# Two hybrid blocks on one core: modulation products kept in one PSUM bank and turned once, attention outputs of the first block in the other

## The chip, the cores and the metric

The kernel runs on one core of one Trainium2 chip. Five engines run side by side and wait for each other through semaphores: TensorE (PE, its weight loads are shown as PEld), VectorE (DVE), ScalarE (ACT), GpSimd (POOL) and SyncE (SP), which here only issues DMAs. Matrix products land in PSUM, which has eight banks of 128 partitions by 512 fp32 values. The metric is the device time in microseconds, the median of the runs shown.

## The reference, cut to what matters

Two model blocks run one after the other on 256 tokens of width 1024. The first has two layers of four mixers (compressed, selected and window attention, stick-breaking, gated linear and forgetting attention), gates, an output product and a squared-ReLU network. The second has two layers whose inputs are scaled and shifted by a modulation vector. That vector depends only on `c`, `c_ctx` and weights, so the kernel computes it during the first block:

```
silu_c  = jax.nn.silu(c)          # one row of 1024
silu_cc = jax.nn.silu(c_ctx)      # one row of 1024
mod_lat = (silu_c @ w_ada[i] + b_ada[i])[:, None, :]    # w_ada[i]: 1024 x 6144
mod_ctx = silu_cc @ w_ada[i] + b_ada[i]
```

For each of the two second-block layers that is a product of two rows with a 1024 x 6144 matrix. It is computed during the first-block layer of the same index, as twelve modulation tiles of 512 columns.

## The kernel before

Each engine's program is written by hand, in the order in which it runs; nothing reorders it. The stages of a first-block layer, by the names of the code:

- **Projections.** Weight tiles of 2 MB come through a ring of slots (`W`). For a product in split precision POOL rounds half a tile (`round_high`, L249), DVE makes its low part (`make_low`, L256), and PE does three matmuls per 128 x 128 piece (L268 to L270).
- **The attention loop.** `for m in range(PAIRS + 1)` has 16 pairs of heads, in turn of the kinds slc, win, fox, sb. Iteration m runs on PE `filler(2m)`, `turned(m-1)` (transposes of probabilities L647, or additions L940 for sb), `scores(m)`, `filler(2m+1)` and `output(m-1)`; after an sb pair the second filler comes ahead of the scores. A filler, called a step below (0 to 31), is 24 matmuls of one piece of the gate product, and behind some of them stands a modulation tile.
- **Branches and output product.** 432 matmuls in a row on PE (`branch_part`, then the `wo` products).
- **The transition to the feed-forward network.** Modulation tiles 10 and 11 (`ada_late`), transposes of the normalised x (`turn_x`), then the first `up` product.
- **Feed-forward network.**

**A modulation tile before.** `ada(n)` is 8 matmuls of a 128 x 32 weight (`silu_c`, whose first two columns hold the two rows, the rest is zero) with 512 moving columns. k mod 4 picks one of four groups of 32 PSUM rows, so that the bank holds four partial sums. ScalarE copies the bank to SBUF (`ada_p`, or `ada_gap` for the two late ones). One step later `turn_ada(n)` multiplies four 128 x 128 pieces of that copy by the first two columns of the constant `sum4`, which adds the four partial sums and turns the result into columns: four matmuls with two moving columns each. ScalarE copies eight columns to `mod` (`take_mod`). fp32 operands of this kind take two passes, so that the trace shows 16 and 8 records for 8 and 4 matmuls.

**PSUM.** The banks are used as four pairs: PROJ, SC (scores), PT (transposes) and OT (outputs). A use takes the next bank of its pair in turn, and its `claim` makes PE wait until the use before the last one, which had the same bank, has been read. The modulation tiles and their turns take their turns in PROJ between the gate fillings; only the late turns take OT. The outputs of the attention alternate between the two banks of OT.

**The ring.** In the loop the gate tiles take slots 0 and 1, the modulation tiles slot 2 alone, so the load of a modulation tile starts when the one before has been used. SP issues in one fixed order (`step_tiles`) and waits in it.

```
ada_steps = [i for i in range(4 * KD - 4) if i % 8 in (1, 4, 6)]     # 1 4 6 9 12 14 17 20 22 25
            if i - 1 in ada_steps:
                turn_ada(ada_steps.index(i - 1), ada_p)
            if i in ada_steps:
                ada(ada_steps.index(i))
```

The prologue loads the fp32 constants in one DMA (L1743); `head_sel` is 1024 of their 2143 columns.

## Time and profile before

| | before |
|---|---|
| median of 3 runs | 2328.16 us |
| lowest, highest | 2326.09, 2331.44 us |
| span of the profiled execution | 2320.9 us |
| PE busy in the span | 2218.5 us (96%) |
| DVE, ACT, POOL busy | 1246.1, 691.2, 480.0 us |
| first-block layers, attention loop | 207 to 397 us, 850 to 1040 us |

The runs' median is 7.3 us above the profiled span; that part lies outside the first and last instruction. A row of the timeline gives start and duration of an instruction, or of a run of like ones, and in brackets how long the engine was idle before it and what ended that. Durations of matmuls overlap with the next one; what a matmul costs PE is the distance from its start to the next start.

### The profile page before, as it was taken

The page shows a single profiled execution, that of the slowest core. Times are in us where ns is not written, and L with a number is a line of the kernel's source. Part 1 is how long each engine was busy: PE and PEld are TensorE (multiplying, and loading weights), DVE is VectorE, ACT ScalarE, POOL GpSimd, SP SyncE. Part 2 cuts the span into 40 slices and gives each one's busy share as a digit, 9 for nine tenths or more (in the row PEclk, how much of TensorE's full clock was granted, in tenths as well). Part 3 has the DMA queues.
Part 4 walks back from the last instruction along what each step waited for, and adds up shares of the span by engine and source line. Part 5 has one row for each costly group of instructions (what it writes and reads, how often), then busy time and mean ns, then how long its engine had stood idle before and what let it go on. Part 6 is the DMA issues. An engine that isn't in the chain of part 4 may idle for free.

```text
span 2320.9 us, 33246 instructions
## 1 busy us (share of the span) xinstructions
PE 2218.5 (96%) x13976; PEld 1801.2 (78%) x13976; DVE 1246.1 (54%) x1690; ACT 691.2 (30%) x1531; POOL 480.0 (21%) x259
## 2 busy tenths in 40 slices
PE   7999999999999999999999998899999999998998
PEld 7998788889888987888898644457888885555887
DVE  5675435855455754348554326664433443466666
ACT  2224444032012244440330357622112013272211
POOL 2222112323312211113233000101111110102332
PEclk9999999999999999999999999999999999999999
DMA  9534665645465346556455303022223232122551
GB/s 269 183 118 153 239 228 164 244 146 219 163 188 186 142 145 236 211 189 240 160 208 218 133 0 115 1 73 91 85 97 108 73 84 72 33 100 99 193 196 58
DMA packets 214281, 340.13 MB, mean 147 GB/s; under 512 B 46540, under 2 KB 82359, under 8 KB 214007
## 3 DMA queue, kind: packets, MB, share of 16 engines
q1 hardware_dynamic: 213040, 334.50, 41.4%
q0 software_dynamic: 944, 3.47, 0.5%
q8 instruction: 112, 1.84, 0.3%
q14 instruction: 35, 0.28, 0.0%
q10 hardware_dynamic: 150, 0.04, 0.0%
HBM read 335.90 MB, written 2.10 MB: 146 GB/s over the span
## 4 chain that ended last, share of the span: by engine, by line
PE 56%; DVE 4%; ACT 4%; issue 1%; POOL 0%; DVEq 0%; ACTq 0%; POOLq 0%
PE bank L2091 14%; PE bank L268 13%; PE bank L270 12%; PE bank L269 12%; PE bank L644 3%; PE bank L2094 2%; DVE ring_low L256 1%; ACT work L1111 1%; ACT work L2458 1%; ACT work L2369 1%; DVE cos L2654 1%; PE bank L647 0%; ACT L1111 0%; DVE work L2667 0%; PE bank L940 0%
## 5 line engine op out<-in xcount | busy, mean ns | idle before, releaser
L269 PE MATMUL bank<-hT_high,ring_low 128*128 128x256 f32 (+1 forms) x2048 | 607.6, 297 | 0.0
L269 PEld LDWEIGHTS bank<-hT_high,ring_low 128*128 128x128 f32 x2048 | 392.2, 192 | 11.7 <-issue 0.7
L249 POOL CAST ring_high<-ring 128x2048 fp32r<-128x2048 f32 (+1 forms) x108 | 204.8, 1897 | 707.1 <-PE bank L270 645.5
L268 PE MATMUL bank<-hT_low,ring_high 128*128 128x256 f32 (+1 forms) x1008 | 294.8, 292 | 9.3 <-DVE ring_low L256 4.6
L256 DVE TENSOR_TENSOR ring_low<-ring,ring_high 128x2048 fp32r<-128x2048 f32 (+1 forms) x108 | 242.3, 2245 | 112.5 <-POOL ring_high L249 112.4
L270 PE MATMUL bank<-hT_high,ring_high 128*128 128x256 f32 (+1 forms) x1008 | 287.2, 285 | 0.0
L249 POOL CAST half_high<-ring 128x2048 fp32r<-128x2048 f32 x64 | 129.3, 2024 | 663.4 <-PE bank L270 464.4
L268 PE MATMUL bank<-ring_low,hidden_high 128*128 128x512 f32 x640 | 254.0, 397 | 0.0
L1111 ACT ACTIVATE work<-bank 128x512 f32<-128x512 f32 (+10 forms) x268 | 121.3, 477 | 367.9 <-PE bank L270 314.9
L268 PEld LDWEIGHTS bank<-hT_low,ring_high 128*128 128x128 f32 (+1 forms) x1008 | 192.1, 191 | 19.9 <-issue 12.5
L256 DVE TENSOR_TENSOR ring_low<-ring,half_high 128x2048 fp32r<-128x2048 f32 x64 | 152.7, 2391 | 99.6 <-POOL half_high L249 99.2
L270 PEld LDWEIGHTS bank<-hT_high,ring_high 128*128 128x128 f32 (+1 forms) x1008 | 191.8, 190 | 0.4
L268 PE MATMUL bank<-hT_low,half_high 128*128 128x256 f32 (+1 forms) x528 | 178.7, 338 | 8.3 <-ACT work L2369 3.5
L270 PE MATMUL bank<-hT_high,half_high 128*128 128x256 f32 (+1 forms) x528 | 176.5, 334 | 0.0
L270 PE MATMUL bank<-half_high,hidden_high 128*128 128x512 f32 x384 | 151.5, 395 | 0.0
L269 PE MATMUL bank<-half_high,hidden_low 128*128 128x512 f32 x384 | 150.7, 392 | 0.0
L2091 PE MATMUL bank<-work,ring 128*128 128x512 f32 (+3 forms) x384 | 139.9, 519 | 4.3 <-DVE work L2550 3.4
L2511 ACT ACTIVATE work<-bank 128x512 f32<-128x512 f32 x48 | 28.7, 598 | 385.5 <-PE bank L270 385.5
L268 PEld LDWEIGHTS bank<-ring_low,hidden_high 128*128 128x128 f32 x640 | 120.2, 188 | 26.8
L2091 PEld LDWEIGHTS bank<-work,ring 128*128 128x128 f32 (+2 forms) x384 | 69.4, 183 | 69.3 <-issue 58.5
L2756 DVE TENSOR_TENSOR hidden_low<-work,hidden_high 128x512 fp32r<-128x512 f32 x48 | 36.2, 755 | 157.5 <-ACT work L2514 157.5
L268 PEld LDWEIGHTS bank<-hT_low,half_high 128*128 128x128 f32 x528 | 100.5, 190 | 20.2 <-ACT work L2369 4.2
(239 smaller groups left out, 4483.3 us busy)
## 6 DMA issues: line engine op xcount, KB each, us to landing
ring<-w_ff SPq DMA_DIRECT2D x32, 2048.0 KB, 8.1
ring<-mlp_w SPq DMA_DIRECT2D x32, 2048.0 KB, 7.9
ring<-w_in SPq DMA_DIRECT2D x30, 2048.0 KB, 7.8
ring<-w_ada SPq DMA_DIRECT2D x20, 2048.0 KB, 7.6
ring<-w_branch SPq DMA_DIRECT2D x24, 512.0 KB, 6.2
ring<-w_in SPq DMA_DIRECT2D x32, 256.0 KB, 4.1
ring<-w_out SPq DMA_DIRECT2D x4, 2048.0 KB, 7.6
work<-w_ada SPq DMA_DIRECT2D x4, 2048.0 KB, 13.9
```

The costliest lines, as they stand in the source:

```text
L249: nc.gpsimd.tensor_copy(self.high(i), self.part(i, False)).then_inc(self.high_made, 1)
L256: nc.vector.tensor_tensor(self.part(i, True), self.part(i, False), self.high(i).bitcast(F32), ALU.subtract)\
L268: nc.tensor.matmul(out, a[0], b[1], start=start, stop=False)
L269: nc.tensor.matmul(out, a[1], b[0], start=False, stop=False)
L270: return nc.tensor.matmul(out, a[0], b[0], start=False, stop=stop)
L644: return nc.tensor.matmul(out, lhsT, rhs, start=start, stop=stop)
L1111: return nc.scalar.activation(out, in_, func, **kw)
L2091: return nc.tensor.matmul(o, lhsT, rhs, start=start, stop=stop)
L2094: return nc.tensor.transpose(o, src, ident)
L2369: return f(o, src, ACT.Copy, **kw)
L2511: f(part, ps[:, :].rearrange("p (a b) -> p a b", a=per), ACT.Relu).then_inc(PROJ.free(name), 1)
L2756: vec.tensor_tensor(hidden_low[:, part, 0:n_tok], hidden[:, part, 0:n_tok], hidden_high[:, part, 0:n_tok].bitcast(F32), ALU.subtract).then ...
```

## The change

The twelve modulation tiles of a layer now add into one kept bank. `silu_c` becomes 54 columns wide, with the two rows at columns 22 and 23 and zeros on both sides. Tile n takes as its weight the 32 columns that begin at 22 - 2n, so that the two rows land in PSUM rows 2n and 2n + 1 of each group of 32, and the other rows of that tile add zeros. The bank is copied once (`ada_sums`) and turned once, with 24 moving columns in place of 2, and four copies of ScalarE spread it over `mod`. The ten in-loop turns, their copies and the ten in-loop copies of tiles are gone.

The kept bank is one of OT, so all attention outputs (`outputs`) take the other one. Banks can be placed by name. The gate fillings have PROJ to themselves. The modulation tiles stand behind steps 3, 6, 8, 11, 14, 16, 19, 22, 24 and 27. The slot of a tile is released by a semaphore of its own (`ada_used`), counted by its last matmul as before. The constant `head_sel` is gone: the four matmuls per fox pair that had it as weight read one column of the identity, repeated with step zero.

```diff
-    ada_steps = [i for i in range(4 * KD - 4) if i % 8 in (1, 4, 6)]
+    ada_steps = [i for i in range(1, 4 * KD - 4) if i % 8 in (0, 3, 6)]
...
-               ["go0", "go1"] + [f"o_{k}{c}" for c in range(HALF_HEADS) for k in ("nsa", "fox", "sb")]
-               + [f"adT{n}" for n in ada_late] + ["rows3"] * (l == DEPTH - 1) + ["down2", "down3"])
+               ["go0", "go1"] + outputs + ["ada", "adT"] + ["rows3"] * (l == DEPTH - 1) + ["down2", "down3"],
+               {"ada": 1, "adT": 0, **{name: 0 for name in outputs}})
...
-                        mm(ps[e][:, at:at + n], head_sel[0:8, 2 * c + e, :], fox_row[0:8, 0:n], False, False)
+                        mm(ps[e][:, at:at + n], ident[0:8, 2 * c + e:2 * c + e + 1].to_broadcast([8, P]), fox_row[0:8, 0:n],
+                           False, False)
...
-            thin(PROJ.claim(pe, f"ada{n}"), silu_c, w, KD).then_inc(PROJ.full, 1)
-
-        def turn_ada(n, src, banks=PROJ):
-            ps = banks.claim(pe, f"adT{n}")
-            PROJ.taken(pe, f"ada{n}")
+            ps = OT.open(pe, "ada") if n == 0 else OT.bank("ada")
+            at = SILU_AT - 2 * n
+            for k in range(KD):
+                rows_of = slice(k % 4 * THIN, k % 4 * THIN + THIN)
+                last = nc.tensor.matmul(ps[rows_of, :], silu_c[:, k, at:at + THIN], w[:, k, :],
+                                        start=n == 0 and k < 4, stop=n == MOD_TILES - 1 and k >= KD - 4,
+                                        skip_group_check=True)
+            if n < MOD_TILES - 1:
+                last.then_inc(ada_used, 1)
+            else:
+                OT.close("ada")
+                last.then_inc(OT.full, 1)
+
+        def turn_ada():
+
+            ps = OT.claim(pe, "adT")
+            OT.taken(pe, "ada")
             for c in range(4):
-                last = mm(ps[:, 2 * c:2 * c + 2], src[:, c * P:(c + 1) * P], K("sum4")[:, 0:2], True, True)
-            last.then_inc(banks.full, 1)
+                last = mm(ps[:, c * THIN:c * THIN + 2 * MOD_TILES], ada_sums[:, c * P:(c + 1) * P],
+                          K("sum4")[:, 0:2 * MOD_TILES], True, True)
+            last.then_inc(OT.full, 1)
...
-            if i - 1 in ada_steps:
-                turn_ada(ada_steps.index(i - 1), ada_p)
...
-        for n in ada_late:
-            take(f"ada{n}", ada_gap[:, n % 2, :])
+        ps = OT.arrived(act, "ada")
+        copy(ada_sums, ps[:, :]).then_inc(OT.free("ada"), 1)
```

What stands on PE in a row, first layer, behind step 2 (the 24 gate matmuls that end it are above the first row). L647 and L658 are transposes, banks 0 and 1 are PROJ, 4 and 5 PT. Before:

```order
L647 MATMUL bank1<-consts,work 128x128 [waits out_free1_12,proj_free1_3]
L647 MATMUL bank1<-consts,work 128x128 x3
L644 MATMUL bank0<-consts,work 128x2 [waits proj_free1_3,proj_free0_2]
L644 MATMUL bank0<-consts,work 128x2 x3
L647 MATMUL bank5<-consts,work 128x128 [waits prob_ready_55,turn_free1_9]
L647 MATMUL bank5<-consts,work 128x128 x2
```

Now:

```order
L658 MATMUL bank0<-consts,work 128x128 [waits out_free1_12,proj_free0_2]
L658 MATMUL bank0<-consts,work 128x128 x3
L658 MATMUL bank5<-consts,work 128x128 [waits prob_ready_56,turn_free1_9]
L658 MATMUL bank5<-consts,work 128x128 x2
L658 MATMUL bank4<-consts,work 128x128 [waits prob_ready_56,turn_free0_8]
```

The turn of tile 0 (128x2) is gone, and the transposes of the gated linear output have bank 0, which step 1 filled, in place of bank 1.

On PE in the second layer, at the transition: the last transposes of x, the turns, the turn of the rows for the norms (128x48) and the first `up` matmul. Banks 6 and 7 are OT. Before:

```order
L647 MATMUL bank1<-consts,work 128x128 [waits proj_free1_3]
L647 MATMUL bank1<-consts,work 128x128 x3
L644 MATMUL bank7<-consts,work 128x2 [waits proj_free0_2,out_free1_12]
L644 MATMUL bank7<-consts,work 128x2 x3
L644 MATMUL bank6<-consts,work 128x2 [waits proj_free1_3,out_free0_11]
L644 MATMUL bank6<-consts,work 128x2 x3
L647 MATMUL bank7<-consts,work 128x48 [waits out_free1_12,rows3_in_119]
L268 MATMUL bank0<-hT_low_79,early_high0_75 128x256 [waits hT_cut_121,proj_free0_2,ff_cut_81]
```

Now:

```order
L658 MATMUL bank1<-consts,work 128x128 [waits proj_free1_3]
L658 MATMUL bank1<-consts,work 128x128 x3
L655 MATMUL bank6<-consts,work 128x24 [waits out_free1_12,out_free0_11]
L655 MATMUL bank6<-consts,work 128x24 x3
L658 MATMUL bank7<-consts,work 128x48 [waits out_free1_12,rows3_in_121]
L282 MATMUL bank0<-hT_low_79,early_high0_75 128x256 [waits hT_cut_123,proj_free0_2,ff_cut_83]
```

Two turns became one, and bank 7, on which the rows' turn waits, was last used by a turn before and is last used by the kept bank now.

## Rows read from the trace of the kernel before

**Rows 1.** Windows: both attention loops. Busy us by engine, clock, DMA share, GB/s.

```profile
207.00:397.00 190.00, 185.93 (x1556) 151.78 (x1554) 83.38 (x182) 95.08 (x256) 31.59 (x17) 1.00 0.63 220
850.00:1040.00 190.00, 185.93 (x1556) 151.83 (x1554) 83.38 (x182) 95.21 (x257) 31.46 (x17) 1.00 0.60 208
```

**Rows 2.** Groups by form, PE, loop of layer 1: count, busy us, mean ns, idle before.

```profile
L644 PE MATMUL bank<-consts,work 128*128 128x2 f32 x80 | 9.6, 242 | 0.1
```

**Rows 3.** Timeline, PE: turns of tiles 1 and 3, and what follows.

```profile
240.88 0.95 PE L644 MATMUL bank<-consts,work 128*128 128x2 f32 x8
241.76 0.44 PE L644 MATMUL bank<-work 128*64 128x256 f32 x2
...
268.81 0.95 PE L644 MATMUL bank<-consts,work 128*128 128x2 f32 x8
269.62 0.85 PE L647 MATMUL bank<-consts,work 128*128 128x128 f32 x6
```

**Rows 4.** Timeline, PE: tile 0 and the start of step 2.

```profile
215.03 1.92 PE L644 MATMUL bank<-ring,silu_c 128*32 128x512 f32 x16 [0.39 <-ACT work L1111]
218.48 0.36 PE L268 MATMUL bank<-hT_low,ring_high 128*128 128x256 f32 x1 [1.52 <-ACT work L1111]
```

**Rows 5.** Timeline, PE: modulation tile 2, sb additions behind step 8, step 9, tile 3.

```profile
245.58 1.92 PE L644 MATMUL bank<-ring,silu_c 128*32 128x512 f32 x16
...
257.25 2.02 PE L940 MATMUL bank<-work,consts 128*128 128x256 f32 x12 [0.26 <-DVE work L1602]
259.03 0.36 PE L268 MATMUL bank<-hT_low,ring_high 128*128 128x256 f32 x1
...
262.03 1.92 PE L644 MATMUL bank<-ring,silu_c 128*32 128x512 f32 x16
```

**Rows 6.** Timeline, DVE: first and last operation between scores(4) and their transposes.

```profile
265.06 0.29 DVE L1607 TENSOR_REDUCE work<-bank 128x1 f32<-128x128 f32 x1 [3.69 <-PE bank L644]
...
268.12 0.35 DVE L1617 TENSOR_SCALAR work<-work 128x256 f32<-128x256 f32 x1
```

**Rows 7.** Issue of one modulation tile in the loop: size, us to landing.

```profile
ring<-w_ada SPq DMA_DIRECT2D x1, 2048.0 KB, 7.6
```

**Rows 8.** Timeline: copy of output o_sb0 on ACT, next claim of an output on PE.

```profile
267.32 0.40 ACT L1111 ACTIVATE work<-bank 128x256 f32<-128x256 f32 x1
...
274.48 1.45 PE L644 MATMUL bank<-work 15*64 15x256 f32 x12
```

**Rows 9.** Groups by form, PEld, loop of layer 1: weights of the fox rows.

```profile
L644 PEld LDWEIGHTS bank<-work,consts 8*128 8x128 f32 x32 | 4.4, 185 | 1.6 <-issue 1.3
```

**Rows 10.** Timeline, transition of the first layer: PE and ACT.

```profile
471.01 0.60 ACT L1111 ACTIVATE work<-bank 128x512 f32<-128x512 f32 x1 [0.42 <-PE bank L644]
...
472.15 1.84 PE L644 MATMUL bank<-consts,work 128*128 128x2 f32 x16
...
475.01 0.36 PE L268 MATMUL bank<-hT_low,early_high 128*128 128x256 f32 x1 [1.02 <-DVE hT_low L1408]
```

**Rows 11.** Timeline, transition of the second layer: PE.

```profile
1114.86 1.84 PE L644 MATMUL bank<-consts,work 128*128 128x2 f32 x16
...
1118.67 0.31 PE L647 MATMUL bank<-consts,work 48*128 48x48 f32 x1 [1.96 <-ACT mod L1111]
1118.91 0.58 PE L268 MATMUL bank<-hT_low,early_high 128*128 128x256 f32 x1
```

**Rows 12.** Windows: behind both transitions. Columns as in rows 1; clock third from last.

```profile
476.00:479.50 3.50, 3.50 (x20) 3.50 (x19) 3.50 (x6) 0.00 (x0) 0.00 (x0) 0.57 0.00 0
...
1118.00:1124.50 6.50, 5.83 (x27) 5.77 (x28) 6.09 (x9) 0.80 (x5) 0.00 (x0) 0.51 0.10 38
```

**Rows 13.** The start: load of the constants, first gemm, DMA rate.

```profile
consts<-f_tables SPq DMA_DIRECT2D x1, 1071.5 KB, 6.2
...
17.81 0.58 PE L268 MATMUL bank<-hT_low,ring_high 128*128 128x256 f32 x1 [3.81 <-DVE ring_low L256]
...
3.00:6.00 3.00, 0.00 (x0) 0.00 (x0) 0.00 (x0) 1.28 (x1) 0.00 (x0) 1.00 1.03 401
```

More of the change, by code:

```diff
@@ L141, with __init__ @@
 class Banks:
-    def __init__(self, pair, uses):
+    def __init__(self, pair, uses, places={}):
         assert len(set(uses)) == len(uses)
@@ L149, in __init__, with open, close @@
         pair.uses += len(uses)
-    def bank(self, name):
-        return self.banks[self.order[name] % self.n]
-    def claim(self, pe, name):
-        i = self.order[name]
-        assert i == self.pair.filled, (name, i, self.pair.filled)
-        self.pair.filled += 1
-        if i >= self.n:
-            pe.wait_ge(self.free_sems[i % self.n], i // self.n)
-        return self.bank(name)
+        self.place, self.earlier = {}, {}
+        for name in uses:
+            self.place[name] = b = places.get(name, pair.turn)
+            pair.turn = (b + 1) % pair.n
+            self.earlier[name] = pair.times[b]
+            pair.times[b] += 1
+    def bank(self, name):
+        return self.banks[self.place[name]]
+    def open(self, pe, name):
+        if self.earlier[name] > 0:
+            pe.wait_ge(self.free_sems[self.place[name]], self.earlier[name])
+        return self.bank(name)
+    def close(self, name):
+        assert self.order[name] == self.pair.filled, (name, self.order[name], self.pair.filled)
+        self.pair.filled += 1
+    def claim(self, pe, name):
+        self.close(name)
+        return self.open(pe, name)
     def arrived(self, eng, name):
@@ L1260, in scalar, with take_mod @@
             f(gl_rstd[:, t], gl_stat[:, t], ACT.Exp, scale=-0.5).then_inc(gl_scale, 1)
-        def take_mod(n, banks=PROJ):
-            ps = banks.arrived(act, f"adT{n}")
-            copy(chip["mod"][:, l * (2 * MODC) + 8 * n:l * (2 * MODC) + 8 * n + 8], ps[:, 0:8]).then_inc(banks.free(f"adT{n}"), 1)
+        def take_mod():
+            ps = OT.arrived(act, "adT")[:, 0:4 * THIN].rearrange("p (c q) -> p c q", c=4)
+            mod = chip["mod"][:, l * (2 * MODC):(l + 1) * (2 * MODC)].rearrange("p (n c s) -> p n c s", n=MOD_TILES, c=4)
+            for c in range(4):
+                last = copy(mod[:, :, c, :], ps[:, c, 0:2 * MOD_TILES].rearrange("p (n s) -> p n s", s=2))
+            last.then_inc(OT.free("adT"), 1)
         def filler(i):
```

41 lines of the change are left out of this document (16 added, 25 removed).

## The prediction

> **What bounds the kernel now.** I read the busy time by stretch first. In the two attention loops, where nearly all of the change lies, PE is busy 185.9 of 190 us in both layers, at the full clock (granted 1.00), while DVE has 83, ACT 95 and POOL 32 us of work [rows 1]. The two loops agree to 0.01 us, so whatever is found in one counts twice. Next I read the waits of PE there: what is left idle is a few single waits of 0.3 to 1.5 us [rows 4, 5]. PE's instruction stream is therefore the path; an instruction that leaves it gives back its whole distance to the next start, unless a load or another engine becomes late. I therefore look for two things: which PE work goes, and which waits have lost so much cover that they appear.
>
> The sum is made against the profiled span of 2320.9 us; what lies around it (7.3 us up to the median) contains none of the changed code, so I subtract the same amount from the median.
>
> **1. Ten turns per layer leave the loop.** Their group has 80 records, ten turns of four matmuls in two passes [rows 2]. Its busy 9.6 us counts the tails that overlap with the next matmul, so I take distances between starts: 240.88 to 241.76 is 0.88 us, 268.81 to 269.62 is 0.81 us [rows 3]. Three of the ten in a layer are of the short kind, seven of the long. That is 3 x 0.81 + 7 x 0.88 = 8.6 us a layer, **17.2 us** for two. None of it was idle time. The ten tiles themselves cost as before: same shapes, same count, about 1.85 us from start to next start when undisturbed (a row's 1.92 less the overlap of its tail [rows 5]).
>
> The trace fixes what a two-column turn costs: 0.88 us for eight passes, 110 ns a pass, although only two columns move [rows 3]. The Trainium skill, page "TensorE: Matmul & The Clock Gate", has two rules that bear on it. Its section "Back-to-back issue gap" puts an isolated matmul of up to 64 columns at about 25 ns, by which the twenty turns would be worth 20 x 8 x 25 ns = 4 us, an estimate. Its section "LDWEIGHTS (loading the stationary operand)" puts a weight load at its columns over 1.2 in ns, 107 ns for 128 columns, which gives 17 us; the row agrees with this one.
>
> **2. The first steps wait less.** Before, tile 0 stands behind step 1 and claims the bank of step 0, then step 2 claims that of step 1, and ACT is late with both: PE idles 0.39 and 1.52 us [rows 4]. Now step 2 meets the first wait (0.39, unchanged), and the transposes of the gated linear output meet the second one a gate step later. A step is 3.0 us (259.03 to 262.03 [rows 5], 0.1 of it the change of tile shape). So they are ready at 215.03 + 2.9 = 217.9, and the bank is free about when step 2 starts before the change, 218.48 [rows 4]: 0.5 us of waiting instead of 1.52. That is 1.0 us a layer, **2.1 us** for two. PE now reaches the transposes of pair 0 some 4 us earlier, where DVE's scaling may not be ready; the bound on the low side is half, 1.0 for both.
>
> **3. Three waits behind sb pairs go.** Behind steps 8, 16 and 24 PE waits 0.26 us for DVE [rows 5]. These steps now carry a modulation tile of 1.85 us, while the turn that went ahead of it was 0.88 us, so the cover grows by about 1.0 us, above 0.26. With the tail of the step that shows in such a wait it is 0.3 us each, six of them: **1.8 us**.
>
> **4. What loses cover.** Three places are narrow, and I cost each at nothing.
> (a) Behind steps 10, 18 and 26 there is neither tile nor turn now. The scores end at 265.07; DVE starts at 265.06 and its last scaling ends at 268.47, 3.4 us later [rows 6]. PE wanted the result at 269.62 and will want it 0.81 us earlier, at 268.81 [rows 3]: 0.34 us of cover is left.
> (b) Tiles stand two steps apart at 6 and 8, 14 and 16, 22 and 24, and slot 2 is loaded only after use. Tile 2 of before stands behind step 6 as tile 1 does now: it starts at 245.58 and ends 1.85 us later, and step 8 ends at 257.25 - 0.26 = 256.99 [rows 5]. That is 9.56 us, and without the 0.88 us of the turn between them 8.7 us. The load takes 7.6 us [rows 7] with nothing ahead of it in SP's order. The gate tile is issued behind it, so its bytes follow in the queue. Margin about 1 us; if it failed it would cost the part over 8.7, six times.
> (c) All outputs use one bank. `output(m)` must wait until ACT has copied the output before it. The copy of o_sb0 ends at 267.7, the next output starts at 274.5 [rows 8], and with a turn of 0.81 us less between them 6.0 us of cover stay. ACT also copies an output before it touches the probabilities that the next one needs, so the new wait can never be the last one.
> The fox rows change their weight from eight real columns of a table to one repeated column. Their loads take 185 ns, no more than others of 128 columns [rows 9]; I cost this at nothing, with a bound of double the load, 64 x 0.185 = 12 us worse.
>
> **5. The transitions.** In the first layer PE is ahead of the others: behind the turns it idles 1.02 us, and the `up` product starts when DVE has the low parts [rows 10]. DVE waits there for ACT, which starts on the halves of hT after its copy of the last tile, 471.01 to 471.5 [rows 10]; that copy stays, at the same time. So one turn less gives nothing: its 0.9 us turn into idling. In the second layer the rows' transpose waits 1.96 us for ACT to free the bank of a turn, which ACT does only after all of hT [rows 11]. The bank is now that of the tiles, freed ahead of hT. The `up` product then starts as in the first layer, 475.01 - 472.15 = 2.86 us after the first turn, at 1117.72 instead of 1118.91 [rows 10, 11]: **1.2 us**.
>
> **6. The clock behind the transitions.** After PE had idled 1.02 us the granted clock fell for 3.0 us (0.57 over the window of 3.5, between 2.4 and 1.2 GHz); after 1.96 us it fell for 5.7 us (0.51 over 6.5) [rows 12]. In the first layer PE will now idle about 2.1 us ahead of `up`, like the second before. I take the second layer's case: 2.7 us more at half speed, **a loss of 1.4 us**; the other end is no loss. The second layer keeps its own. The Trainium skill says on the page "TensorE: Matmul & The Clock Gate", section "What's actually happening", that the throttled state is the default and that activity releases it; the trace agrees with its 0.57 and 0.51 behind idle stretches.
>
> **7. The start.** The constants shrink by 1024 of 2143 columns, 512 KB of 1071.5, and move at 401 GB/s: 1.3 us [rows 13]. ACT's first operation waits for them, and from it the chain of squares, norm, transposes and hT leads to the first gemm at 17.81 [rows 13]; the tiles' bytes behind the constants come earlier too. I take **1.3 us**; the low bound is 0.
>
> Sum: 17.2 + 2.1 + 1.8 + 1.2 - 1.4 + 1.3 = 22.2 us, so 2328.2 - 22.2 = **2306.0 us**, 1.0% faster.
>
> **The rivals.**
> *A. The cover is too thin.* PE gives up its work, but waits appear in its place: (b) by 1 us six times, (a) by 0.5 us six times, no gain at the start (1.3), another dip of the clock of 3 us at half speed (1.5). That takes 6 + 3 + 1.3 + 1.5 = 11.8 us: 2318. For it: all margins are under 1 us. Against it: steps 28 to 31 carry no tile or turn already and add only waits as in [rows 5].
> *B. Slower: one bank for the outputs.* There are 24 outputs of which 22 follow another. If ACT fell behind so that each had to wait for the copy of the one before, with a price of 1.2 us (one or two copies of 0.4 us [rows 8] and one more operation of that length in front of them), the loops would lose 26.4 us: 2332. It decides from 1.0 us per output, where it eats the 22.2. Against it stand 6.0 us of cover in (c) and ACT at half load in [rows 1].
> *C. Nothing comes of it.* The turns would only fill holes that something slower makes, a load or POOL's rounding, and the loop keeps its 190 us: 2328.2 less items 5 and 7, plus item 6, 2327. Against it: PE is idle for only 4 of 190 us, with named waits [rows 1, 4, 5].
> *D. More than forecast.* The clock falls less often (the loss of item 6 stays away and one other dip of 3 us goes, 1.4 + 1.5): 2303.
>
> **How the numbers follow.** Forecast with D: 0.84; A: 0.09; B: 0.03; C: 0.04. The forecast with its bounds (start 0 to 1.3, first steps 1.0 to 2.1, clock -3 to +3, (a) and (b) up to 2 together, and the 2.5 us by which the runs themselves differ) reaches from 2299 to 2312; that alone holds 8 in 10, so the range needs none of the rivals. About 0.2% (4.7 us) is what a measurement of this kernel can tell from no change. Faster by more takes the forecast, A and D: 0.93; within it C: 0.04; slower B: 0.03.
>
> **What would show it.** In the profile of the changed kernel: two-column matmuls gone, and one group of 24 columns with 16 records in all; each loop, from its first step to the 432 matmuls of the branches, shorter by 10.5 us; no wait of L940's successor behind steps 8, 16, 24, but still one before the branches; a wait of about 0.5 us in place of 1.52 at the transposes of the gated linear output; no wait for `mod` ahead of the 48-column transpose; a granted clock near 0.5 for about 6 us behind both transitions; the first gemm at 16.5 us. It would be wrong if modulation tiles wait for DMA, if transposes wait for DVE's L1617 in steps 10, 18, 26, if an output waits for ACT's copy, or if the fox rows' weight loads take more than 185 ns.

## The result, and the profile after

| | before | after |
|---|---|---|
| median, first comparison | 2327.12 us (4 runs) | 2294.45 us (4 runs) |
| lowest, highest | 2322.89, 2331.44 us | 2288.33, 2300.05 us |
| ratio, 95% interval | | 0.9859 (0.9837 to 0.9882) |
| span of the profiled execution | 2320.9 us | 2294.1 us |
| instructions of PE, ACT | 13976, 1531 | 13800, 1493 |

The change saves 32.7 us by the medians of this comparison (25 to 36 us by the interval of a second one below). I had predicted 2306.0 us with a range of 2299 to 2312: faster was right, but the time lies 5 us below the range. Before looking for a cause it helps to know the spread: single executions of before lay anywhere from 2315 to 2335 us, so a trace is one draw. I therefore compare the stages over two traces of before and three of after. A ratio below is always to executions of before taken beside the kernel in question.

| stage, mean of its traces in us | before | after | difference | predicted |
|---|---|---|---|---|
| start to first gemm | 17.8 | 17.5 | -0.3 | -1.3 |
| projections, layer 1 | 190.2 | 190.2 | 0 | 0 |
| loop, layer 1 | 189.5 | 178.8 | -10.7 | -10.55 |
| loop, layer 2 | 189.6 | 178.5 | -11.1 | -10.55 |
| branches and output product, both | 131.6 | 131.3 | -0.3 | 0 |
| last `wo` matmul to first `up`, layer 1 | 12.2 | 12.7 | +0.5 | 0 (+1.4 clock) |
| the same, layer 2 | 12.4 | 11.7 | -0.7 | -1.2 |
| first `up` of layer 1 to loop of layer 2 | 375.6 | 373.8 | -1.8 | 0 |
| first `up` of layer 2 to the end | 1204.1 | 1197.4 | -6.7 | 0 |
| sum of the rows | | | -31.1 | -22.2 |

The +1.4 us of clock is my item 6; it is in the predicted sum and was meant to fall behind the first `up`. The loops came out as forecast. Nearly all of the miss lies in the last two rows, nearly all of whose instructions the change does not touch. That is what the experiments had to explain.

The windows of the two loops after, from the first step to the branches (columns as in rows 1):

```profile
209.28:387.97 178.69, 176.64 (x1473) 142.78 (x1473) 88.74 (x182) 87.29 (x233) 31.18 (x17) 1.00 0.63 221
840.45:1018.92 178.47, 176.46 (x1473) 142.67 (x1472) 88.71 (x182) 87.29 (x233) 31.18 (x17) 1.00 0.66 233
```

PE has lost 9 us of busy time against the windows of [rows 1], and it idles 2 us where it idled 4. The groups by form, PE, first of the whole span and then of the loop of layer 1:

```profile
L655 PE MATMUL bank<-consts,work 128*128 128x24 f32 x16 | 1.9, 259 | 0.0
...
L655 PE MATMUL bank<-work 128*64 128x256 f32 x64 | 10.4, 404 | 0.0
```

```profile
L655 PEld LDWEIGHTS bank<-work,consts 8*128 8x128 f32 x32 | 4.4, 184 | 1.6 <-issue 1.3
```

In place of the 80 two-column records of [rows 2] in each loop there are 16 of 24 columns in the kernel. PE never waits ahead of the outputs (128*64): one bank is enough. The fox rows' weight load takes 184 ns, where [rows 9] has 185.

The timeline of PE at the first steps, at step 8, and at both transitions:

```profile
216.84 0.36 PE L282 MATMUL bank<-hT_low,ring_high 128*128 128x256 f32 x1 [0.38 <-ACT work L1134]
...
220.20 1.31 PE L658 MATMUL bank<-consts,work 128*128 128x128 f32 x10 [0.30 <-ACT work L1134]
...
252.78 1.92 PE L1000 MATMUL bank<-ring,silu_c 128*32 128x512 f32 x16
254.63 2.02 PE L952 MATMUL bank<-work,consts 128*128 128x256 f32 x12
...
453.93 1.92 PE L1000 MATMUL bank<-work,silu_c 128*32 128x512 f32 x16
458.41 1.09 PE L658 MATMUL bank<-consts,work 128*128 128x128 f32 x8 [2.55 <-DVE work L1415]
459.43 3.22 PE L1000 MATMUL bank<-work,silu_c 128*32 128x512 f32 x16
...
466.70 0.52 PE L282 MATMUL bank<-hT_low,early_high 128*128 128x256 f32 x1 [1.88 <-DVE hT_low L1430]
...
1093.58 0.97 PE L655 MATMUL bank<-consts,work 128*128 128x24 f32 x8
1094.48 0.26 PE L658 MATMUL bank<-consts,work 48*128 48x48 f32 x1
1096.52 0.36 PE L282 MATMUL bank<-hT_low,early_high 128*128 128x256 f32 x1 [1.78 <-DVE hT_low L1430]
```

The first waits are 0.38 and 0.30 us where [rows 4] has 0.39 and 1.52. The sb additions behind step 8 start without the 0.26 us of [rows 5]. The 48-column transpose no longer waits 1.96 us for `mod` [rows 11], yet the wait ahead of `up` is now 1.78 us.

### The profile page after: what moved, and what is told of

It is laid out like the page before. It is cut to its first block, busy times and chain, and to the rows that moved or that the text cites. A ratio compares the mean times of both kernels' runs of the same rounds, so it can differ in the third digit from the quotient of the medians.

```text
span 2294.1 us, 32812 instructions
## 1 busy us (share of the span) xinstructions
PE 2195.1 (96%) x13800; PEld 1780.6 (78%) x13800; DVE 1259.4 (55%) x1690; ACT 676.0 (29%) x1493; POOL 482.8 (21%) x259
## 4 chain that ended last, share of the span: by engine, by line
PE 56%; DVE 4%; ACT 3%; issue 1%; POOL 0%; DVEq 0%; ACTq 0%; POOLq 0%
PE bank L2113 14%; PE bank L282 13%; PE bank L284 13%; PE bank L283 12%; PE bank L655 2%; PE bank L2116 2%; DVE ring_low L270 1%; PE bank L1000 1%; ACT work L2480 1%; ACT work L2391 1%; DVE cos L2676 1%; ACT work L1134 1%; PE bank L658 0%; DVE work L2689 0%; PE bank L952 0%
## 5 line engine op out<-in xcount | busy, mean ns | idle before, releaser
L1134 ACT ACTIVATE work<-bank 128x384 f32<-128x384 f32 (+11 forms) x246 | 109.4, 466 | 360.8 <-PE bank L284 311.7
## 6 DMA issues: line engine op xcount, KB each, us to landing
work<-w_ada SPq DMA_DIRECT2D x4, 2048.0 KB, 13.2
```

The costliest lines, as they stand in the source:

```text
L1134: return nc.scalar.activation(out, in_, func, **kw)
```

## What sets 6 to 9 us of it: where the work area lies

Consecutive matmuls of the first layer's `down` product have 512 moving columns and no waits between them. Here are the first and the last of 384, PE's timeline, in before and in after:

```profile
567.49 0.39 PE L268 MATMUL bank<-ring_low,hidden_high 128*128 128x512 f32 x1
...
656.85 0.39 PE L270 MATMUL bank<-late_high,hidden_high 128*128 128x512 f32 x1
```

```profile
559.10 0.43 PE L282 MATMUL bank<-ring_low,hidden_high 128*128 128x512 f32 x1
...
646.81 0.39 PE L284 MATMUL bank<-late_high,hidden_high 128*128 128x512 f32 x1
```

That is 89.36 us for 383 distances, 233.3 ns each, against 87.71 us and 229.0 ns. The code of this product is the same. A distance below means from start to start at full clock; unless a product is named, it is averaged over the 2832 split-precision matmuls of this shape in the kernel: 232.7 ns in before (659.1 us in all), 230.9 ns in after (654.0 us). These 5.1 us are a term that my sum did not have at all. Unless said otherwise, the product named below is this one, the `down` product of the first layer.

**The same kernels again.**

> The kernel before, unchanged, so that its own spread is seen. Theory S (spread): the profiled span of before, 2320.9 us, belonged to a short execution; the median is near 2327 us, executions lie up to 4 us on either side, and a second trace of the same code shows stretches of half clock at other places or of other lengths, and 512-column matmuls whose distance in the feed-forward network is not always 233.3 ns. Rival F (fixed): the two traces agree to 1 us at every stage, the distance is 233.3 ns again, and the 6.5 us that the 512-column matmuls lost in all between the traces of before and after belong to the change. Ratio to before: 1.000 within 0.002 by both.

> The changed kernel, unchanged. Theory S: ratio 0.985 to 0.989, its trace shows the stable parts again (each attention loop shorter by 10.85 us, no wait of 0.68 us ahead of modulation tile 10, DVE's tensor-tensor operation in the making of the cosine table at about 2.1 us instead of 0.43), while the half-clock stretches at the transitions move. Rival F: those stretches stand as in the first trace, one from 459.9 us and one from 466.7 us in the first layer and none at the transition of the second.

Measured: before again 2326.15 us, ratio 0.9992 (0.9974 to 1.0011), distance 232.7 ns; after again 2295.77 us, ratio 0.9868 (0.9845 to 0.9891), distance 230.9 ns. Both theories were half right. The distance is fixed to 0.1 ns from trace to trace of one kernel, so it belongs to the kernel (F). The stretches of half clock and their lengths move (S): one of 3.4 us near 183 us stands in both traces of before and in none of after, and the transition of the second layer had one of 6.8 us in one trace of before and of 3.4 us in the other, none in the first of after and one of 3.4 us in its second.

**Only the table `head_sel` gone.**

```diff
-        "head_sel": np.repeat(np.eye(P)[:, :8], P, axis=1),
...
-                        mm(ps[e][:, at:at + n], head_sel[0:8, 2 * c + e, :], fox_row[0:8, 0:n], False, False)
+                        mm(ps[e][:, at:at + n], ident[0:8, 2 * c + e:2 * c + e + 1].to_broadcast([8, P]), fox_row[0:8, 0:n], False, False)
```

> Before, with one part of the change alone: the table head_sel gone and the fox rows reading a repeated column of the identity. Theory C (collision): ACT starts 1.5 us earlier, the first gemm 0.6 us; POOL's rounding that began at 39.34 begins near 38.5 us, stands beside DVE's tensor-tensor operation of the cosine table, which then takes 2.1 us instead of 0.43, and PE waits 1.4 us for ring_low near 45 us. The layer-1 attention loop then starts about 1 us later than in before in spite of the earlier start, and the time is 2328 us (ratio 0.9995 to 1.001). Rival L (load only): the delay in the changed kernel came from its larger silu_c; here the start stays 1 us ahead and the time falls by 1 us (0.9995). My prediction had minus 1.3 us for it. The fox rows' weight loads stay at 185 ns by both.

Measured: 2324.95 us, ratio 0.9996 (0.9982 to 1.0011), first gemm at 17.25 us, distance 233.1 ns. No collision in this trace: DVE's operation took 0.42 us, the first gemm came 0.6 us earlier and the loop began 3.1 us earlier than in before, as rival L had it and not theory C. As shown below, that collision is met or missed by chance, so one trace does not decide between them. The run gives the reference for the next one: all tensors lie 4096 bytes lower, and the time is that of before.

**The table `silu_c` wider, nothing else.** On top of the edit above:

```diff
-        chip["silu_c"] = sb("silu_c", [P, KD, THIN])[:, :, :]
+        chip["silu_c"] = sb("silu_c", [P, KD, 54])[:, :, 0:THIN]
```

> As consts_only, and the table silu_c allocated 54 columns wide instead of 32, while only its first 32 are used: no instruction differs, but every tensor of the work area lies 704 bytes further. In the feed-forward networks of the traces of before, the 2832 matmuls with 512 moving columns in split precision take 232.7 ns from start to start on average (659.1 us in all), and in both traces of the changed kernel 230.9 ns (654.0 us), the same number in each repetition. Theory P (placement): where the operands lie in SBUF sets this distance; here it falls from the 233.1 ns of consts_only to 230.9 ns, 6 us in all: 2319 us, ratio to before 0.997 (consts_only has 0.9996). Rival Q (program): the distance goes with the instruction stream of PE, and stays at 233.1 ns; ratio 0.9996.

Measured: **2318.05 us, ratio 0.9957 (0.9940 to 0.9974)**, distance 230.9 ns. The first layer's `down` product in this kernel:

```profile
562.29 0.39 PE L267 MATMUL bank<-ring_low,hidden_high 128*128 128x512 f32 x1
...
649.99 0.39 PE L269 MATMUL bank<-late_high,hidden_high 128*128 128x512 f32 x1
```

87.70 us as in after, with the instructions of consts_only, which took 89.36. Theory P holds: placement alone moves the distance, and Q falls. 704 unused bytes in each partition give 0.4% (7 us by the medians, 9 by the ratios), somewhat more than the 6 us that the distance explains.

**Gaps ahead of the work area.** The edit is one line in the changed kernel, with 80, 16, 48 or 32 words (32 together with the first modulation tile behind step 1). In shift_all192 the 48 words go into the table of constants instead, ahead of the ring.

```diff
+        sb("gap", [P, 80])
         work_base = nc.sbuf_base
```

> The changed kernel with 320 unused bytes in each partition ahead of the work area, so that the work area lies 1024 bytes further than in consts_only, not 704. Theory P with the rule that the distance repeats each 1024 bytes: 233.1 ns as in consts_only, 6 us longer than the changed kernel: 2301 us, ratio to before 0.989. Rival within P (another period): some other value between 229 and 236 ns. Rival Q: 230.9 ns as in the changed kernel, 2295 us, ratio 0.9865.

> The changed kernel with 64 unused bytes ahead of the work area: it lies 768 bytes beyond that of consts_only, where the changed kernel has 704 (230.9 ns a matmul on average) and after_gap320 1024 (233.1 ns). Theory P256 (the distance repeats with 256 bytes or less): 233.1 ns, since 768 is three times 256. Theory P512 (it repeats with 512 or 1024 bytes only): another value, between 226 and 236 ns. By 2832 matmuls, 1 ns is 2.8 us.

> The changed kernel with 192 unused bytes ahead of the work area, 896 bytes beyond consts_only. Theory P128 (repeats with 128 bytes or less): 233.1 ns in this one and in after_gap64. Otherwise one of the two differs from 233.1 ns; if this one lies below 230.9 ns, it is a placement that beats the changed kernel, by 2.8 us for each ns.

> As first_tile_at_1, with 128 unused bytes ahead of the work area: 832 bytes beyond consts_only. So far 0, 768 and 1024 bytes gave 232.8 to 233.1 ns, 704 gave 230.9 and 896 gave 231.1 ns, so the distance repeats with 256 bytes or less, and 832 leaves the untried remainder 64. By symmetry of 64 and 192 I expect 230.9 ns and the time of first_tile_at_1, 2294 us. Rival (no symmetry): a value between 229 and 233.1 ns, 5 us less to 6 us more.

> The changed kernel with 48 unused columns in the table of constants, so that the ring, the transposed x and the work area all lie 192 bytes further, and their distances from each other stay. Theory Rel (relative placement counts): 230.9 ns as in the changed kernel. Theory Abs (the place of the work area modulo 256 bytes counts, wherever the ring lies): 704 + 192 = 896 leaves 128, as in after_gap192, with 226 to 227 ns in the first block's down products and 231.1 ns on average; if the ring's own place counts as well, a third value. The constants are 24 KB longer, 0.06 us.

| kernel | work area beyond consts_only, bytes | remainder by 256 | distance | median, us (runs) | mean granted clock |
|---|---|---|---|---|---|
| consts_only | 0 | 0 | 233.1 ns | 2324.95 (12) | 0.988 |
| after_gap64 | 768 | 0 | 232.8 ns | 2309.26 (1) | 0.986 |
| after_gap320 | 1024 | 0 | 233.1 ns | 2303.74 (5) | 0.988 |
| first_at_1_gap128 | 832 | 64 | 231.5 ns | 2293.94 (5) | 0.990 |
| after_gap192 | 896 | 128 | 231.1 ns | 2292.78 (1) | 0.992 |
| after | 704 | 192 | 230.9 ns | 2294.45 (4) | 0.989 |
| shift_all192 | 896, ring moved as well | 192 from the ring | 230.9 ns | 2291.8 (1) | 0.993 |

after_gap320 has the ratio 0.9901 (0.9887 to 0.9916): **320 bytes more take back 8 us** of the changed kernel's gain, by the medians 2295.77 and 2303.74. The single executions of three rows differ in clock, so their times rank nothing; their distances can be compared. The average distances of 0, 768 and 1024 against 704 and 896 fit a repetition with 256 bytes and not with 128. The remainder 64 is not the mirror of 192 that I expected: 231.5 ns, and 232.0 in the first layer's `down` product instead of 229.0. In shift_all192 the work area lies where it lay in after_gap192, but the ring moved along, and the distance stays that of after: what counts is where the tensors lie relative to each other. The `down` product of the three kernels, PE's timeline (after_gap320, after_gap192, shift_all192):

```profile
557.84 0.39 PE L282 MATMUL bank<-ring_low,hidden_high 128*128 128x512 f32 x1
...
647.20 0.39 PE L284 MATMUL bank<-late_high,hidden_high 128*128 128x512 f32 x1
```

```profile
556.79 0.40 PE L282 MATMUL bank<-ring_low,hidden_high 128*128 128x512 f32 x1
...
643.62 0.39 PE L284 MATMUL bank<-late_high,hidden_high 128*128 128x512 f32 x1
```

```profile
557.81 0.39 PE L283 MATMUL bank<-ring_low,hidden_high 128*128 128x512 f32 x1
...
645.51 0.40 PE L285 MATMUL bank<-late_high,hidden_high 128*128 128x512 f32 x1
```

89.36, 86.83 and 87.70 us for the same product. Its weights come from the work area, and of its moving data the low part from the ring and the rounded part from the work area. All three matmuls of a piece change with the gap (from consts_only to silu_wide 234.0, 230.0, 236.0 ns become 229.3, 228.4, 229.2), also those whose own operands all lie in the work area; which pair of addresses matters is not shown.

Placement does not fix every product by itself. With remainder 0 the `down` product of the second layer took 231.3 ns in both traces of before and in no_turns, but 233.3 in consts_only, late_own_bank, after_gap64 and after_gap320; that of the first layer took 231.1 in after_gap64 and 233.3 in the six others. With remainder 192 both took 229.0 in all eight traces. What chooses between the two values at remainder 0 is open.

The Trainium skill, page "SBUF — State Buffer", section "Who interferes with whom", says that only one pair of ports, shared by VectorE and GpSimd, causes contention, and that TensorE reads weights and moving data through ports of its own; these runs show TensorE's rate depending on placement, and the measurement decides.

How much of the time is this? The stretch from the second layer's first `up` to the end took 1202.0 to 1210.2 us in the seven traces with remainder 0 and 1195.0 to 1200.4 in the eight with remainder 192; the groups do not overlap, and their means are 7.9 us apart. The distance of the 512-column matmuls accounts for 4.0 of them. The rest goes with the clock: over this stretch the granted clock averaged 0.985 in the seven traces and 0.990 in the eight.

The clock can be taken out of whole executions too, since time and mean granted clock are known for each. Around the mean of its own kernel, an execution whose granted clock is 0.001 lower takes 1.7 us longer; before, for example, took 2315.0 us at 0.992 and 2334.8 us at 0.985. So most of the spread between executions is the clock. Brought to the same clock of 0.988 by that slope (an estimate, good to about 1 us), the means are 2325.5 us for consts_only and 2318.4 for silu_wide, and 2297.8 for after again and 2304.1 for after_gap320. That is 7.1 and 6.3 us for placement, close to the 6.1 that the distance gives in both; the rest of the measured 8 to 9 us is a granted clock 0.001 lower. Why the clock was lower with the slower placement, or whether that was chance, was not settled.

## The terms of the sum, one by one

**Turns alone.** The edit takes the turns and the copies out and leaves bank order otherwise alone (ScalarE zeroes `mod` once in the prologue, so this kernel leaves out the modulation values of tiles 0 to 9):

```diff
-        if i - 1 in ada_steps:
-            step_fills.append(f"adT{ada_steps.index(i - 1)}")
...
-            if i - 1 in ada_steps:
-                turn_ada(ada_steps.index(i - 1), ada_p)
...
-            if i - 1 in ada_steps:
-                take_mod(ada_steps.index(i - 1))
```

> Before without the ten turns in the attention loop of each layer and without ScalarE's ten copies behind them: the modulation values of tiles 0 to 9 are not computed and stay zero. The tiles are computed and copied as before and still take their bank. My prediction's item 1 has 17.2 us for this (0.81 and 0.88 us each): each loop 180.9 us instead of 189.5, ratio 0.9926, 2309.5 us. Rival C of the prediction (the turns only fill holes that something slower makes): the loop stays above 187 us and the ratio above 0.998.

Measured: 2308.55 us, ratio 0.9921 (0.9908 to 0.9934), 18.4 us less than before by the ratio. Its two loops:

```profile
205.92:386.99 181.07, 177.16 (x1473) 142.92 (x1473) 87.65 (x182) 92.43 (x243) 31.32 (x17) 1.00 0.66 230
843.13:1024.22 181.09, 177.17 (x1473) 142.90 (x1472) 87.24 (x182) 92.42 (x243) 31.32 (x17) 1.00 0.63 218
```

8.46 us less in each, 16.9 us in all where item 1 had 17.2. Rival C falls. PE still waits 0.38 and 1.52 us at the first steps and 0.25 us behind each sb pair there, so the 2.3 to 2.6 us by which the loops of after are shorter still (178.8 and 178.5 us, means of three traces) are items 2 and 3 (2.0 us a loop forecast).

**The tiles in their old places.** The changed kernel with `ada_steps` of before:

> The changed kernel with the modulation tiles behind the steps of before (1, 4, 6, 9, ... instead of 3, 6, 8, 11, ...). By items 2 and 3 of my prediction: PE waits 0.26 us again behind steps 8, 16 and 24 (0.3 us each with the tail), and the waits ahead of step 2 or of the gated linear transposes change by up to 1 us; each loop 0.9 to 1.9 us longer than the 178.5 to 179.1 us of the changed kernel, 2 to 4 us in all: 2298 us, ratio to before 0.9878. Rival (places do not matter): the waits stay hidden, ratio 0.9865.

Measured: 2295.49 us, ratio 0.9878 (0.9855 to 0.9900); loops 179.2 us both. PE's timeline has the wait behind step 8 again, and none at all at the first steps:

```profile
251.43 0.81 PE L952 MATMUL bank<-work,consts 128*128 128x256 f32 x3 [0.27 <-DVE work L1624]
```

So the new places hide three waits of 0.26 us and leave open first waits of 0.7 us, which the old places hid: 0.1 us in their favour by the rows, 0.4 and 0.7 us by the loops. The 1.52 us of [rows 4] went because the tiles left PROJ, not because of their new places, and a tile hides the wait that it stands in front of.

**Both at once.**

```diff
-    ada_steps = [i for i in range(1, 4 * KD - 4) if i % 8 in (0, 3, 6)]
+    ada_steps = [1] + [i for i in range(4, 4 * KD - 4) if i % 8 in (0, 3, 6)]
```

> The changed kernel once more, as the reference for the three others of this call: ratio to before 0.9865, and 230.9 ns between the starts of the 512-column matmuls, as in its other two traces. The first wait of the loops, ahead of step 2 and of the gated linear transposes, is 0.4 + 0.3 us in both layers.

> The changed kernel with modulation tile 0 behind step 1 instead of step 3, all others left. With all tiles in their old places the waits of 0.4 and 0.3 us at the start of the loop were gone and the four waits of 0.26 us for DVE behind sb pairs were there. Theory W (each tile covers the wait behind its step, 1.85 us of work against 0.26 to 0.7): now both kinds are hidden, the loops take 178.4 and 178.0 us, 0.5 us less than the changed kernel each, 1 us in all: ratio 0.9861. Rival: the first tile's load is late at step 1, so that PE waits for DMA, 0.5 us or more; ratio 0.9865 or above.

Measured on one chip: after 2292.04 us, ratio 0.9879 (0.9857 to 0.9901); with the first tile behind step 1 **2290.34 us, ratio 0.9860 (0.9832 to 0.9888)**, the lowest median of the study, though the intervals overlap. The loops took 178.3 and 177.6 us against 178.6 and 178.5. The second loop gains its 0.9 us; the first loses part of it to a load. Here it is, and below it the same tile in the second trace of after:

```profile
337.45 1.92 PE L1000 MATMUL bank<-ring,silu_c 128*32 128x512 f32 x16 [0.66 <-DMA ring<-w_ada]
```

```profile
336.96 1.92 PE L1000 MATMUL bank<-ring,silu_c 128*32 128x512 f32 x16 [0.51 <-DMA ring<-w_ada]
```

This is the narrow place (b): I had 1 us of margin from a load of 7.6 us, but the median load of `w_ada` took 9.3 us in the first loop of after's first trace. In that trace the same tile starts at 339.51 after 0.10 us of idling. Of the ten traces with tiles two steps apart at 22 and 24, eight wait for this load, by 0.4 to 1.0 us, once, in the first loop; no trace with the old places does. So the margin is gone, the wait is not owed to the tile at step 1, and it costs about 0.5 us.

**A bank of its own for the late tiles.** Before, with tiles 10 and 11 in OT:

```diff
-            thin(PROJ.claim(pe, f"ada{n}"), silu_c, w, KD).then_inc(PROJ.full, 1)
+            banks = OT if n in ada_late else PROJ
+            thin(banks.claim(pe, f"ada{n}"), silu_c, w, KD).then_inc(banks.full, 1)
...
```

> Before, with the two late modulation tiles (10 and 11) in the banks of OT instead of the pair PROJ, which the output product has just filled. Theory B (bank): the wait of 0.68 us ahead of tile 10 is a wait for DVE to read a bank of the output product; with a bank of its own the tile starts 0.2 to 0.3 us behind the last matmul, 0.7 us earlier in each layer, as in the changed kernel. The transposes behind wait for DVE anyway, so that this gives nothing at the end by itself: PE waits 0.7 us more for the transposes, ratio 1.000 within 0.001. Rival (gain kept): the 0.7 us stay until the first up product, 1.4 us in all, ratio 0.9994.

Measured: 2327.24 us, ratio 1.0004 (0.9993 to 1.0015). PE's timeline, first before, then this kernel:

```profile
463.85 1.92 PE L644 MATMUL bank<-work,silu_c 128*32 128x512 f32 x16 [0.68 <-DVE x_sb L1653]
468.00 1.09 PE L647 MATMUL bank<-consts,work 128*128 128x128 f32 x8 [2.22 <-DVE work L1393]
```

```profile
463.46 1.92 PE L644 MATMUL bank<-work,silu_c 128*32 128x512 f32 x16
```

Tile 10 starts 0.32 us behind the last `wo` matmul instead of 1.08 us, in after as well; my prediction had overlooked that the kept bank removes this wait. But it is worth nothing at the end, since the transposes behind it wait for DVE: they start 4.80 us after the last `wo` matmul in layer 1 of all three traces of after, with the tile at 0.33, and 5.2 us after it in both of before, with the tile at 1.08.

## The collision of DVE with POOL

In the first trace of after the projections lost what the shorter constants had gained. POOL's rounding is the CAST in its timeline. Here are DVE, POOL and PE in that trace, and then the same DVE operation in the second trace:

```profile
38.50 2.13 DVE L1816 TENSOR_TENSOR work<-work 128x256 f32<-128x256 f32 x1
```

```profile
38.46 1.90 POOL L263 CAST ring_high<-ring 128x2048 fp32r<-128x2048 f32 x1 [4.91 <-DMA ring<-w_in]
```

```profile
45.28 0.36 PE L282 MATMUL bank<-hT_low,ring_high 128*128 128x256 f32 x1 [1.41 <-DVE ring_low L270]
```

```profile
38.93 0.43 DVE L1816 TENSOR_TENSOR work<-work 128x256 f32<-128x256 f32 x1
```

The operation that began 0.04 us after POOL's rounding took 2.13 us instead of 0.43, until the rounding was over; everything behind it on DVE came 1.7 us later, and PE waited 1.41 us. In [rows 13] the constants set when the weight tiles land, and the landing sets when POOL rounds: a faster start moves the rounding onto another DVE operation. I tried to step out of its way, with DVE's four operations on the angle (`cos_angle`) moved behind its eight additions:

```diff
             else:
+                if l == 0:
+                    chip["cos_angle"]()
                 Y.make_low(nc, dve, 4)
...
```

> The changed kernel, with the four DVE operations that prepare the cosine put behind DVE's eight additions for the compressed keys, so that the tensor-tensor operation meets no rounding of POOL. Theory C: it takes 0.43 us again, the low part of the fifth tile ends 1.4 us earlier, PE's wait of 1.41 us at 45.28 goes, and the projections end 1.3 us earlier: 2293.0 us, ratio to before 0.9853 when the changed kernel has 0.9859. Rival L: the operation is slow because of what it reads, and stays at 2.1 us wherever it stands; the time does not move or rises by up to 1 us.

Measured: 2295.16 us, ratio 0.9861 (0.9835 to 0.9886), no gain over after again (0.9868). DVE and POOL in it:

```profile
39.26 1.89 DVE L1818 TENSOR_SCALAR work<-work 128x256 f32<-128x256 f32 x1
```

```profile
39.10 1.90 POOL L263 CAST ring_high<-ring 128x2048 fp32r<-128x2048 f32 x1 [6.43 <-DMA ring<-w_in]
```

Now another operation, of another kind, is the one caught. So L falls (it is not what the operation reads), and C holds as a mechanism, but the remedy was wrong: the rounding comes when the load lands, at 38.5, 39.8 and 39.5 us in the three traces of after, and DVE has an operation there in either order. The Trainium skill, page "SBUF — State Buffer", section "SBUF: two separate sides", describes a pair of ports that VectorE and GpSimd share as an exclusive lock held for a whole instruction; the trace agrees, with 2.13 and 1.89 us where 0.43 and 0.29 us are usual. Operations that read PSUM were not held: the additions of L1445 (L1467 in after) ran beside a rounding at full speed in before, 8 in 1.94 us.

The traces hold many more such meetings. Over all 17, 467 TENSOR_TENSOR operations on 128x512 elements with both inputs in SBUF began during a rounding, more than 0.3 us before its end. Each ended after it, in 0.94 to 2.39 us where 0.69 is usual. Of the same size but with one input in PSUM, 89 began during one and took their 0.69. The kind of operation matters as well: 26 RECIPROCAL operations on 128x1 elements, with both sides in SBUF, took their usual 0.16.

The same thing sets the transitions. DVE's scaling of a row block, and POOL, in after's second layer:

```profile
1087.31 2.14 DVE L1415 TENSOR_SCALAR work<-x_sb,work 128x1024 f32<-128x1024 f32 x1
...
1091.84 0.75 DVE L1415 TENSOR_SCALAR work<-x_sb,work 128x1024 f32<-128x1024 f32 x1
```

```profile
1085.16 3.73 POOL L263 CAST late_high<-ring 128x2048 fp32r<-128x2048 f32 x2 [4.62 <-DMA ring<-w_ff]
```

Two roundings in a row last until 1088.9 and hold the scaling; it takes 2.14 us instead of 0.75, and the first transposes, which PE awaits there, come 4.8 to 5.3 us after the last `wo` matmul. In traces where the scaling slipped between the roundings they came after 3.6 to 4.0 us. That is 0.8 to 1.7 us a layer, and it was not removed here.

## Why the prediction was too cautious, point by point

Two steps of it failed. The sum had no term for where the tensors lie, which was worth 6 to 7 us at the same clock. And its clock term did not come: item 6 charged 1.4 us for a longer stretch at half clock behind `up` of layer 1, but both traces of before have 3.4 us there and the three of after 3.4, 3.4 and none. Over the whole kernel the clock moved the other way: the executions of after again had a granted clock of 0.989 on average against 0.987 of before beside them, worth some 3 us of gain by the slope above. The steps on PE's work in the loops held.

**Turns (17.2 us): right.** 16.9 us with the turns alone. The price came from distances between starts in the trace, at a place where nothing waited.

**First waits and sb waits (2.1 + 1.8 us): 1 us short.** By the loops of after against those of no_turns it is 4.9 us. The reason given for the first waits was half wrong: it was the bank, not the place. (By its own rows the item gives 1.52 - 0.55 = 0.97 us a layer, 1.9 for two and not 2.1.)

**Narrow places (nothing): nearly right.** Place (b) was named as a sign of being wrong, and it did fail: tile 8 waits for its load in the first loop of most traces, for about 0.5 us. Item 4 had taken the load's 7.6 us from the old places. There the median stays so (7.6 us in before, 7.7 in after_old_places), but with the new places it is 9.2 to 9.5 us in the three traces of after. What slows the load there was not tested. Rival A did not come otherwise, nor B: no output waits for a copy, which [rows 8] had said with 6 us of cover.

**Transitions (-1.2, +1.4 us): in part.** The wait for `mod` in the second layer went, 0.7 us arrived. In the first layer the wait ahead of `up` grew from 1.02 to 1.88 us, as the 2.1 forecast had it, and this cost nothing by itself. The 0.5 us lost there on average are clock: two of the three traces of after have a stretch at half clock ahead of `up`, and the transition took 13.1 and 13.2 us in them against 11.8 us in the third. That a longer wait lengthens the stretch at half clock was a wrong rule: the windows of after in layer 1 (twice) and in layer 2, clock third from last,

```profile
460.00:463.00 3.00, 3.00 (x18) 0.69 (x11) 0.92 (x2) 0.79 (x4) 0.00 (x0) 0.50 1.05 408
467.00:470.00 3.00, 3.00 (x15) 3.00 (x15) 3.00 (x8) 0.76 (x6) 0.00 (x0) 0.50 0.00 0
1096.00:1102.00 6.00, 5.48 (x46) 5.51 (x47) 6.00 (x12) 1.68 (x10) 0.00 (x0) 1.00 0.19 73
```

show 1.2 GHz ahead of the last turn and again behind `up` after waits of 2.55 and 1.88 us, and 2.4 GHz throughout behind waits of 2.71 and 1.78 us in the second layer. From one trace I had taken the length of a fall as a function of the idling; it differs between executions of one kernel. The reading was off as well: 0.51 over 6.5 us [rows 12] is 6.4 us at half clock, not 5.7, so by its own rule item 6 should have been a loss of 1.7 us.

**Start (1.3 us): a quarter of it.** The first gemm came 0.3 us earlier on average. ACT did start 1.5 us earlier (5.87 instead of 7.43 us), but then waited 0.95 us for PE's transpose of the parameter rows, which waits for loads of its own.

**Missing: the placement.** This term, put at nothing without a reason, is the main miss: 5 to 6 us by the distances, 6 to 7 at equal clock by silu_wide and after_gap320, and 8 to 9 as measured there with the clock in it. The diff showed it in one number, `SILU_W` in the allocation of `silu_c`, and I had read that number as memory only. It also shows what the change itself is worth: with the work area in the old remainder (after_gap320) the ratio is 0.9901, 23 us, or 21 us at equal clock, where the forecast had 22.2. That the two agree so well is in part luck, since the clock term and most of the start did not come as forecast, while items 2 and 3 gave 1 us more.

**The reference point.** I took 7.3 us between median and profiled span for time outside the span. Each execution's time is 1.8 us above its own span, in both kernels; the rest is that the profiled execution was one of the short ones. It did not change the forecast saving, but it would have told me that the median of three runs was uncertain by several us.

**Open.** Which property of two addresses sets the distance; whether the lower clock that went with the slower placement is its effect; and why the `down` product of layer 2 takes 694 ns for three matmuls in before (230, 233, 231) but 700 ns in late_own_bank (234, 230, 236), whose placement is the same.

## What to carry to other kernels

Price what leaves an engine that hardly ever idles by the distance between starts, and it comes back to within a few per cent. Treat any change in the size of an on-chip table as a change of every tensor behind it: to know what an edit is worth by itself, restore the old placement with an unused gap, and to gain for nothing, try a few gaps (here 320 bytes moved the time by 8 us). Judge a stage by several traces, since loads, half-clock stretches and collisions of DVE with POOL fall differently each time, and compare whole executions at the same granted clock.

## What the runs showed of the hardware

Matmuls of 512 columns in one product, the first layer's `down`, followed each other after 226.7 (after_gap192), 229.0 (after), 231.1 (after_gap64), 232.0 (first_at_1_gap128) or 233.3 ns (before, after_gap320) at the full clock, by where the work area lay, and to 0.1 ns the same in each trace of one kernel. At remainder 0 a product of this kind took one of two values, about 231.3 or 233.3 ns, in kernels of the same placement. A DVE addition or scaling with all operands in SBUF that begins during one of POOL's roundings ends only after it (2.13 us for 0.43, 1.89 for 0.29, 2.14 for 0.75). One that reads PSUM runs on, and so does a RECIPROCAL on 128x1. Between executions of one kernel, 0.001 less of mean granted clock went with 1.7 us more, and stretches at half clock came and went at the same place.
